# Dilated attention groups sorted by token remainder: from two classes of 128 tokens to four of 64

## The reference, cut to what matters

```python
DIL_PAIRS = ((128, 1), (512, 4), (2048, 16))
...
        for gi, (w, d) in enumerate(DIL_PAIRS):
            steps = jnp.arange(n_keys[gi]) * d
            idx = t[:, None] + w - steps[None, :]
            ...
            logits = jnp.where((t[:, None] - steps[None, :]) >= 0, logits, NEG_INF)
            lse = jax.nn.logsumexp(logits, axis=-1)
            p = jnp.exp(logits - lse[..., None]).astype(v.dtype)
            outs.append(jnp.einsum('bhqj,bqjhd->bhqd', p, v_g, preferred_element_type=jnp.float32))
            lses.append(lse)
        wts = jax.nn.softmax(jnp.stack(lses, axis=0), axis=0)
```

## Time and profile before

| what | value |
|---|---|
| median of 3 runs | 972.23 us (971.95 to 972.58) |
| profiled execution, first to last instruction | 970.2 us |
| time outside that span, median less span | 2.0 us |
| TensorE busy in the span | 965.0 us, 99% |
| VectorE busy | 624.8 us, 64% |
| ScalarE busy | 593.2 us, 61% |
| granted TensorE clock | 1.000 |

### The profile page before, as it was taken

How to read it: one execution, slowest core, us unless ns; L and a number is a source line. 1 busy time by engine, 2 the same in 40 slices (tenths; PEclk the granted TensorE clock), 3 DMA queues, 4 the chain that set the end, 5 groups by cost and what they waited for, 6 DMA issues and landing times.

```text
span 970.2 us, 13113 instructions
## 1 busy us (share of the span) xinstructions
PE 965.0 (99%) x4938; PEld 796.5 (82%) x4938; DVE 624.8 (64%) x770; ACT 593.2 (61%) x920; POOL 15.8 (2%) x28
## 2 busy tenths in 40 slices
PE   9999999999999999999999999999999999999998
PEld 7888788888888887888888888888888888888887
DVE  5776766555556767665655555977685667786654
ACT  7777665454545666564545455877667768857571
POOL 2000000000000000000000000000000000000000
PEclk9999999999999999999999999999999999999999
DMA  9545266756564553457666655555534444446651
GB/s 312 155 141 188 87 214 194 242 173 216 173 198 143 181 173 131 131 168 248 222 205 195 226 185 173 174 174 174 174 129 136 150 133 153 130 148 204 207 180 44
DMA packets 106223, 169.37 MB, mean 175 GB/s; under 512 B 4213, under 2 KB 65863, under 8 KB 106177
## 3 DMA queue, kind: packets, MB, share of 16 engines
q1 hardware_dynamic: 103600, 161.23, 50.6%
q0 software_dynamic: 2240, 7.40, 2.4%
q10 hardware_dynamic: 336, 0.10, 0.0%
HBM read 167.56 MB, written 1.16 MB: 174 GB/s over the span
## 4 chain that ended last, share of the span: by engine, by line
PE 99%; DVE 0%; ACT 0%; issue 0%; POOL 0%; DVEq 0%; ACTq 0%; POOLq 0%
PE acc L524 14%; PE acc L526 14%; PE acc L525 13%; PE acc L609 12%; PE pair_ps L526 8%; PE pair_ps L524 8%; PE pair_ps L525 7%; PE acc L991 3%; PE acc L675 3%; PE turn_ps L765 2%; PE turn_ps L627 1%; PE acc L792 1%; PE acc L575 1%; PE pair_ps L748 1%; PE pair_ps L744 1%; PE turn_ps L524 1%
## 5 line engine op out<-in xcount | busy, mean ns | idle before, releaser
L2064 DVE TENSOR_TENSOR w_lo<-w_raw,w_hi 128x2048 fp32r<-128x2048 f32 (+3 forms) x154 | 343.2, 2231 | 122.5 <-ACT w_hi L1316 122.1
L1316 ACT ACTIVATE w_hi<-w_raw 128x2048 fp32r<-128x2048 f32 (+3 forms) x154 | 286.5, 1864 | 83.0 <-PE acc L526 41.0
L524 PE MATMUL acc<-w_hi,uT_hi 128*128 128x512 f32 (+3 forms) x440 | 173.0, 393 | 1.0 <-ACT qkv L1403 1.0
L526 PE MATMUL acc<-w_hi,uT_lo 128*128 128x512 f32 (+3 forms) x440 | 167.9, 381 | 0.0
L525 PE MATMUL acc<-w_lo,uT_hi 128*128 128x512 f32 (+3 forms) x440 | 167.4, 381 | 0.0
L524 PE MATMUL pair_ps<-w_hi,uT_hi 128*128 128x512 f32 x320 | 126.5, 395 | 0.0
L526 PE MATMUL pair_ps<-w_hi,uT_lo 128*128 128x512 f32 x320 | 124.9, 390 | 0.0
L525 PE MATMUL pair_ps<-w_lo,uT_hi 128*128 128x512 f32 x320 | 124.6, 389 | 0.0
L524 PEld LDWEIGHTS acc<-w_hi,uT_hi 128*128 128x128 f32 x440 | 82.7, 188 | 18.7 <-issue 4.5
L526 PEld LDWEIGHTS acc<-w_hi,uT_lo 128*128 128x128 f32 x440 | 82.6, 188 | 16.1
L525 PEld LDWEIGHTS acc<-w_lo,uT_hi 128*128 128x128 f32 x440 | 82.8, 188 | 13.7
(11 more groups left out here) (311 smaller groups left out, 1358.3 us busy)
## 6 DMA issues: line engine op xcount, KB each, us to landing
w_raw<-in_w_in SPq DMA_DIRECT2D x46, 1024.0 KB
w_raw<-in_w_gate SPq DMA_DIRECT2D x44, 512.0 KB
w_raw<-in_w_up SPq DMA_DIRECT2D x44, 512.0 KB
w_raw<-in_w_down SPq DMA_DIRECT2D x22, 1024.0 KB
w_raw<-in_w_out SPq DMA_DIRECT2D x12, 1024.0 KB
w_raw<-in_w_qkv SPq DMA_DIRECT2D x16, 512.0 KB
w_raw<-in_w_branch SPq DMA_DIRECT2D x6, 1024.0 KB
w_raw<-in_w_qkv SPq DMA_DIRECT2D x4, 1024.0 KB
```

The costliest lines, as they stand in the source:

```text
L524: mm(o, xh, wh[:, k, :], start=first and k == 0, stop=False)
L526: done = mm(o, xl, wh[:, k, :], start=False, stop=last and k == len(kts) - 1)
L1316: activation(w_hi[:, slot, 0:width], w_raw[:, slot, 0:width], ACT.Copy).then_inc(hi_done, 1)
L2064: v.tensor_tensor(w_lo[:, slot, 0:width], w_raw[:, slot, 0:width], w_hi[:, slot, 0:width].bitcast(f32), ALU.subtract).then_inc(lo_done, 1)
```

## The change

The tokens of the two class groups are sorted by their remainder by four. A class c = 2b + m has 64 tokens. Its logits are a 64 by 64 product that goes to output partitions 64b, and the two classes m lie beside each other. All four pairs of a group are handled at one place: 32 products for the logits (`class_logits`), 8 transposes (`turn_class_probs`), 32 products for the values (`class_values`), where m selects the rows of the array and the bank, and 8 transposes of the outputs. ACT and DVE have functions of their own for it. The window stage no longer has class work. The statistics and the bias rows are laid out to match, with more and smaller transfers on POOL, and POOL copies a `selector` for `sort_scales`.

```diff
         def in_turn(x, i):
-            return x[:, 2 * i:2 * i + 2, :].rearrange("p k (i c) -> p k c i", c=TB)
+            return x[:, 2 * i:2 * i + 2, :].rearrange("p k (i c) -> p k c i", c=4)
...
-                pool.dma_start(bias[:, g, :, 0:P], bass.AP(class_rows.tensor, 8 * (g - 2) * (S - 1),
-                                                           [[1, P], [S - 1, 8], [1, P]])).then_inc(bias_full[g], 16)
-
+                for b in range(2):
+                    pool.dma_start(bias[HD * b:HD * b + HD, g, :, 0:HD],
+                                   bass.AP(class_rows.tensor, 8 * (g - 2) * (P - 1), [[1, HD], [P - 1, 8], [1, HD]]))\
+                        .then_inc(bias_full[g], 16)
+
+            nc.gpsimd.tensor_copy(selector.rearrange("p c (b i) -> p c b i", b=TB),
+                                  ident[:, :].rearrange("p (i c) -> p c i", c=4).unsqueeze(2).broadcast_to([P, 4, TB, 32]))\
+                .then_inc(selector_full, 1)
...
+                for b in range(2):
+                    pool.dma_start(stat_rows[i].rearrange("(i b m) c -> b i m c", b=2, m=2)[b],
+                                   class_stats[HD * b:HD * b + HD, i, :, :, :].rearrange("p m k h -> p m (k h)"))\
+                        .then_inc(stat_stored, 16)
...
+            def class_logits(pair0, turn0):
+
+                pe.wait_ge(qkT_read, turn0 + 4)
+                for t in range(4):
+                    for m in range(2):
+                        for b in range(2):
+                            c0 = HD * (2 * b + m)
+                            for j in range(2):
+                                q, k = [qkT[HD * j:HD * j + HD, t, S * i + c0:S * i + c0 + HD] for i in range(2)]
+                                o0 = P * t + HD * m
+                                done = mm(pair_ps[HD * b:HD * b + HD, j, o0:o0 + HD], q, k, start=True, stop=True,
+                                          skip_group_check=True)
+                done.then_inc(logit_done, 4)
+
+            def turn_class_probs(pair0):
+
+                for j in range(2):
+                    pe.wait_ge(prob_done, pair0 + 2 * (j + 1))
+                    for t in range(4):
+                        done = transpose(turn_ps[:, j, P * t:P * t + P],
+                                         class_probs[:, j, t, :, :].rearrange("p m k -> p (m k)"), ident[:, :])
+                    done.then_inc(prT_done, 2)
+
+            def class_values(pair0, v_tile):
+
+                pe.wait_ge(prT_act, pair0 + 4)
+                pe.wait_ge(prT_dve, pair0 + 4)
+                pe.wait_ge(out_read, pair0)
+                pe.wait_ge(out_copied, pair0 - 16)
+                for t in range(4):
+                    for b in range(2):
+                        for m in range(2):
+                            for j in range(2):
+                                c0 = P * t + HD * b
+                                done = mm(class_outs[m][HD * j:HD * j + HD, c0:c0 + HD],
+                                          v_tile[b][HD * m:HD * m + HD, t, HD * j:HD * j + HD],
+                                          class_turned[HD * m:HD * m + HD, j, c0:c0 + HD], start=True, stop=True,
+                                          skip_group_check=True)
+                done.then_inc(out_done, 4)
...
-            def project_last_and_attend(kind, copied, v_tile, v_before):
+            def project_and_attend_classes(widths, copied, v_tile, v_before=None, following=None, classes=False):
...
                     if s == 2:
-                        turn_probs(kind, 1, pair0)
+                        turn_class_probs(pair0)
 
                 def end(s):
                     if s == 0:
-                        two_logits(kind, 0, pair0, turn0)
-                        two_values(kind, 2, pair0 - 4, v_before)
-                    if s == 1:
-                        turn_probs(kind, 0, pair0)
+                        class_logits(pair0, turn0)
+                        if v_before:
+                            two_values("last", 2, pair0 - 4, v_before)
+                    if s == 1 and v_before:
                         turn_outputs(1, pair0 - 4, head_outs)
                     if s == 2:
-                        two_logits(kind, 2, pair0, turn0)
                         pe.wait_ge(acc_read, copied)
-                        two_values(kind, 0, pair0, v_tile)
+                        class_values(pair0, v_tile)
                     if s == 3:
-                        turn_probs(kind, 2, pair0)
-                    if s == 4:
-                        turn_probs(kind, 3, pair0)
-                        turn_outputs(0, pair0, head_outs)
+                        turn_class_outputs(pair0)
...
                     if s == 1:
                         two_logits(kind, 0, pair0, turn0)
-                        two_values(kind_before, 2, pair0 - 4, v_before)
                     if s == 2:
                         turn_probs(kind, 0, pair0)
-                        turn_outputs(1, pair0 - 4, head_outs)
...
+            def class_exponentials(j, pair0):
+
+                act.wait_ge(max_done, pair0 + 2 * (j + 1) - 4)
+                for t in range(4):
+                    for m in range(2):
+                        head = slice(2 * t + j, 2 * t + j + 1)
+                        pr = class_probs[:, j, t, m, :]
+                        done = activation(pr, pr, ACT.Exp, bias=negmax8[:, m, head], accum_out=total8[:, m, head])
+                done.then_inc(prob_done, 2)
...
+            def class_maxima(pair0, table):
+
+                dve.wait_ge(logit_done, pair0 + 4)
+                dve.wait_ge(prT_done, pair0)
+                for j in range(2):
+                    for m in range(2):
+                        done = v.scalar_tensor_tensor(class_probs[:, j, :, m, ::-1],
+                                                      pair_ps[:, j, :].rearrange("p (t m k) -> p t m k", t=4, m=2)[:, :, m, ::-1],
+                                                      HD ** -0.5, table[:, j:8:2, 0:HD], ALU.mult, ALU.add)
+                    done.then_inc(logit_read, 2)
+                for j in range(2):
+                    dve.wait_ge(logit_read, pair0 + 2 * (j + 1))
+                    v.tensor_reduce(negmax8[:, :, j:8:2].rearrange("p m t -> p t m"), class_probs[:, j, :, :, :],
+                                    op=ALU.max, axis=AX.X, negate=True).then_inc(max_done, 2)
```

More of the change, by code:

```diff
@@ L184, in branch_banks @@
             return acc[2:4] if (i, half) != (0, 0) else acc[0:2]
-        groups = ("last", "classes")
+        class_probs = flat_logit[:, 0:1024].rearrange("p (j t m k) -> p j t m k", j=2, t=4, m=2)
+        class_turned = prT[:, :, :, :].rearrange("p a b c -> p (a b c)")[:, 0:1024].rearrange("p (j c) -> p j c", j=2)
+        class_outs = acc[2:4]
+        selector = bias[:, 2, 4:8, P:P + HD]
         v_tiles = [[qkv[:, 2, blk, :].rearrange("p (t c) -> p t c", t=4) for blk in range(TB)],
@@ L194, in prob_tile @@
         def prob_tile(kind, t):
-            return pair_ps if (kind in groups and t % 2) or (kind, t) == ("band", 5) else turn_ps
+            return pair_ps if (kind == "last" and t % 2) or (kind, t) == ("band", 5) else turn_ps
         def out_bank(kind, t):
-            if kind in groups:
+            if kind == "last":
                 return acc[3][:, S * (t % 2):S * (t % 2) + S]
@@ L744, in logits @@
                     mm(logit_tile(kind, t)[:, j, 0:128], q[:, 0:128], k[:, 0:128], start=True, stop=True)
[L745 to L748, removed]
+                    done = mm(logit_tile(kind, t)[:, j, 128:384], q[:, 128:256], k, start=True, stop=True)
                 done.then_inc(logit_done, 1)
@@ L795, in values, with turn_outputs @@
                 done.then_inc(out_done, 1)
-            def turn_outputs(half, pair0, outs):
+            def turn_outputs(half, pair0, outs, bank=acc[2]):
                 pe.wait_ge(out_copied, pair0 + 2 * (half + 1) - 16)
-                pe.wait_ge(out_read, pair0 + 2 * half)
+                pe.wait_ge(out_read, pair0 + (2 * half if bank is acc[2] else 0))
                 for t in range(2):
                     for blk in range(TB):
-                        done = transpose(acc[2][:, S * t + P * blk:S * t + P * blk + P], outs[half][:, t, P * blk:P * blk + P],
+                        done = transpose(bank[:, S * t + P * blk:S * t + P * blk + P], outs[half][:, t, P * blk:P * blk + P],
@@ L807, in two_logits, with turn_class_outputs @@
+            def turn_class_outputs(pair0):
+                pe.wait_ge(out_copied, pair0 + 4 - 16)
+                for half in range(2):
+                    turn_outputs(half, pair0, head_outs, class_outs[half])
             def two_logits(kind, t, pair0, turn0):
@@ L847, in sort_scales, with project_and_attend @@
                 pe.wait_ge(row_scale, 6)
-                for i in range(TB):
-                    for blk in range(TB):
```

(27 more changed lines are left out.)

200 lines of the change are left out of this document (96 added, 104 removed).

## The result

| | before | after |
|---|---|---|
| median of the runs of the comparison | 972.03 us (971.95 to 972.58, 5 runs) | 965.70 us (965.51 to 965.92, 5 runs) |
| profiled execution, first to last instruction | 970.2 us | 963.7 us |
| class stretch: first class product to last head transpose, the same work in both | 119.56 us | 113.16 us |

The ratio is 0.9934, 95% interval 0.9923 to 0.9945: 6.3 us less, where 5.9 less (966.3 us) was forecast, and inside the range. The span fell by 6.5. Of that, 6.4 lie in the class stretch.

The account below looks back on a forecast made before the run. TensorE, busy in 99% of the span, was taken to bound the kernel; -1.76 - 3.30 - 0.0 - 1.0 + 0.2 = -5.9 us gave a span of 964.3, plus 2.0 to the median: 966.3 us, range 965.2 to 969.5.

Parts of the forecast that it names:

- transposes, 16 fewer: Turning class probabilities on TensorE: two halves of four transposes per group instead of four pairs, 0.11 us each, -1.76 us.
- three insertions of class products alone: Three places between projections holding only class logits and values: each from 2.41 to 1.31 us, -3.30 us in all.
- mixed insertion: End of the first unit, first class group, class logits ahead of two value pairs that stay: 0.0 us.
- window stage: A class value block of 1.03 us leaves with its 0.09 switch, an exit of 0.10 stays: -1.0 us.
- new wait: TensorE at the third unit of the second class group, waiting on ACT's acc copy behind eight exponentials: +0.2 us.
- Part 2: Insertions of class products alone: 16 steps of 0.06 us, four records each, plus 0.16 fixed, 1.12 a block; -3.30 us.
- Rival A: Class product blocks: starts cost, not columns; a set of four costs 0.12, a block 2.08, 970.1 us; chance 0.20.
- rival C: Class product blocks: the four quarters don't overlap, steps of 0.24 in place of 0.06, 977.8 us; chance 0.04.
- Part 3: Mixed insertion of the first class group 0.0 us; class value block leaving the window stage -1.0 us.
- Part 1: Transposes of class probabilities, 0.11 us each with nothing on top, 16 fewer in two groups: -1.76 us.
- Part 4: Work moved to ACT and DVE lies beside projections; no slack at the second class group's third unit: +0.2 us.
- first reading: TensorE's view of waits: two waits over the whole span, 2.1 us in all, neither in attention work.

## Why the prediction was right

The bound was read rightly, and the working holds term by term, against the class stretch (-6.4):

| term | forecast | measured | from |
|---|---|---|---|
| transposes, 16 fewer | -1.76 | -1.8 | what the other terms leave of 6.4; read as insertions, the places with transposes from the first class product to the last went from 7.04 to 5.29 us in all (-1.75); four transposes more cost 0.43 to 0.48 |
| three insertions of class products alone | -3.30 | -3.36 | 3 x (1.29 - 2.41) |
| mixed insertion | 0.0 | -0.1 | 2.54 less 2.65 |
| window stage | -1.0 | -1.0 | 1.62 less 2.64 |
| new wait | +0.2 | +0.2 | 8.52 less 8.30 |
| stall at 802.33, before | not seen | -0.3 | 3.25 less 2.95 |

All insertions of the class stretch together went from 31.4 to 25.2 us, read place by place like those above; the stall gone and the new wait added make that 6.4.

- Part 2's choice, 0.06 for a step of four records, was the one that mattered, and it was an argument by two halves: row halves overlap, column halves overlap, so quarters do. No row could show it beforehand. Measured: 0.058, with 0.16 fixed. Rival A (2.08 us a block) and rival C (0.16 + 16 x 0.24 = 4.0) are excluded by the block itself. The Trainium skill's rule of about 25 ns from start to start ("TensorE: Matmul & The Clock Gate", Part 1) gave 1.6 us a block and 969.0; here four starts lie within 20 ns, and the measurement decides. The step of 0.058 us for each quarter is the floor seen here.
- Part 3's 0.0 was 0.1 too high, within its coarse switch of 0.09. Part 1 left the price of a place out, 0.02 to 0.04 for each of four places fewer.
- Part 4 had the place of the new wait right, and the engine. Its size was an allowance and fell right by luck: the sum itself had ACT's copy done at 5.45 and TensorE there at 5.5, no wait, and 0.2 was put for "no slack". The copy was done 5.53 behind the end of the logits (782.52 - 776.99). The cover for the rest held: in the class stretch nothing else of ACT, DVE or POOL reached TensorE.
- What the prediction had wrong is its first reading: "over the whole span there are two waits ... neither of them in attention work". The view of waits was read for matmuls only. The one of the weight loads lists more, most of them outside the class stretch and the same after, and one in it: 0.3 us on ACT's two reads of the gate bank, in the second class group. It is half of the 0.6 us by which the span undercut the forecast (963.7 against 964.3). The rest is the mixed insertion, 0.1, and small parts of the other terms. The distance from span to median was 2.0 as forecast (965.70 - 963.7).

Moving DVE's maximum forward is free and removes the last 0.2 us of wait. No run here beat the change measurably.

## What to carry to other kernels

When small matrix products fill only a part of the array, order them so that successive ones go to different quarters: the same 64 records took 1.09, 1.24, 1.84 or 3.33 us by order alone, and put them at few places, since each costs 0.35 us for the way in and out. On a kernel bound by TensorE, look for stalls shorter than a matmul's record in the distances of starts; the waits of matmuls don't list them, and those of the weight loads named one of the two met here. What a wait is for is read from the source, not from a tile's name. And before a stage gets all its exponentials at one place, count ACT's queue up to the next bank that TensorE wants: behind that point, each further us is paid in full.

## What the runs showed that was not expected

- By the count of steps, TensorE starts records past others that wait for a busy quarter. With runs of four records on a quarter, 64 records still took 19 steps (16 at best, 49 if only neighbours overlapped); with runs of sixteen, three steps at each change carry both quarters. A limit of two waiting records for each quarter fits all orders tried; that is a fit, not a sight of the queue.
- An in-place copy of 64 columns on ACT takes 0.16 us back to back, an exponential of the same shape with its accumulator read 0.33.
- Moving ACT's 0.62 us copy behind the two reads of the gate bank gave TensorE 0.3 us, with the same work on every engine.
